# First attention of a two-block transformer kernel: turns, scores and values in one visit behind every second slab

## The reference

```
s = einsum('bnqhd,bnkhd->bhnqk', q, kb) * scale + rel_bias_band(rel_table)
s = where(valid, s, NEG_INF)
p = softmax(s, axis=-1)
o = einsum('bhnqk,bnkhd->bnqhd', p, vb)
```

## Time and profile before

| | us |
|---|---|
| three runs | 929.07, 929.38, 929.80 |
| median | 929.38 |
| profiled execution | 929.6 |
| its span | 927.8 |
| busy: TensorE, VectorE, ScalarE, GpSimd | 919.3, 599.4, 490.1, 303.6 |

### The profile page before, as it was taken

How to read it: one execution, slowest core, us unless ns; L and a number is a source line. 1 busy time by engine, 2 the same in 40 slices (tenths; PEclk the granted TensorE clock), 3 DMA queues, 4 the chain that set the end, 5 groups by cost and what they waited for, 6 DMA issues and landing times.

```text
span 927.8 us, 16744 instructions
## 1 busy us (share of the span) xinstructions
PE 919.3 (99%) x6268; PEld 833.8 (90%) x6268; DVE 599.4 (65%) x849; ACT 490.1 (53%) x765; POOL 303.6 (33%) x140
## 2 busy tenths in 40 slices
PE   9999999999999999999999999999999999999997
PEld 8999877788899999888999998888889889999886
DVE  6968967756657777723777775357476866666523
ACT  6788456743555444444644444446364754445441
POOL 0000000000044554544254556554341044445442
PEclk9999999999999999999999999999999999999999
DMA  8756575445556567796566666645513356666661
GB/s 258 248 182 183 175 230 179 133 159 185 178 170 194 182 188 235 238 257 197 182 189 197 195 209 203 222 151 159 175 63 93 113 153 190 196 199 190 189 200 67
DMA packets 132797, 169.49 MB, mean 183 GB/s; under 512 B 16731, under 2 KB 88446, under 8 KB 132614
## 3 DMA queue, kind: packets, MB, share of 16 engines
q1 hardware_dynamic: 132582, 168.67, 58.6%
q10 hardware_dynamic: 160, 0.07, 0.0%
HBM read 167.61 MB, written 1.10 MB: 182 GB/s over the span
## 4 chain that ended last, share of the span: by engine, by line
PE 92%; DVE 3%; issue 1%; DMA 1%; ACT 1%; SPq 1%; POOL 1%; DVEq 0%; POOLq 0%; ACTq 0%
PE acc L904 14%; PE acc L906 14%; PE acc L905 14%; PE acc L962 14%; PE acc L964 14%; PE acc L966 14%; PE tp L980 3%; PE acc L1315 1%; DVE w_lo L1400 1%; DMA w_raw<-in_w_ffn_out 1%; PE sc L1270 1%; PE sc L1116 1%; PE tp L1135 1%; PE acc L1048 1%; POOL w_lo L2068 1%
## 5 line engine op out<-in xcount | busy, mean ns | idle before, releaser
L541 ACT ACTIVATE w_hi<-w_raw 128x1024 fp32r<-128x1024 f32 x300 | 316.8, 1058 | 277.1 <-PE acc L906 130.0
L2068 POOL TENSOR_TENSOR w_lo<-w_raw,w_hi 128x1024 fp32r<-128x1024 f32 x106 | 278.4, 2626 | 512.4 <-ACT w_hi L541 512.3
L1400 DVE TENSOR_TENSOR w_lo<-w_raw,w_hi 128x1024 fp32r<-128x1024 f32 x194 | 258.0, 1334 | 200.6 <-ACT w_hi L541 200.1
L962 PE MATMUL acc<-xt_hi,w_hi 128*128 128x256 f32 x1248 | 347.4, 278 | 0.1
L966 PE MATMUL acc<-xt_hi,w_lo 128*128 128x256 f32 x1248 | 346.4, 278 | 0.0
L964 PE MATMUL acc<-xt_lo,w_hi 128*128 128x256 f32 x1248 | 346.4, 278 | 0.0
L962 PEld LDWEIGHTS acc<-xt_hi,w_hi 128*128 128x128 f32 x1248 | 235.2, 188 | 1.4 <-issue 0.9
L966 PEld LDWEIGHTS acc<-xt_hi,w_lo 128*128 128x128 f32 x1248 | 234.6, 188 | 0.0
L964 PEld LDWEIGHTS acc<-xt_lo,w_hi 128*128 128x128 f32 x1248 | 234.4, 188 | 0.1
L904 PE MATMUL acc<-w_hi,hid_hi 128*128 128x512 f32 x264 | 103.2, 391 | 0.1
L905 PE MATMUL acc<-w_hi,hid_lo 128*128 128x512 f32 x264 | 102.9, 390 | 0.0
(11 more groups left out here) (228 smaller groups left out, 949.7 us busy)
## 6 DMA issues: line engine op xcount, KB each, us to landing
w_raw<-in_ffn_w_gu SPq DMA_DIRECT2D x172, 256.0 KB
w_raw<-in_w_in SPq DMA_DIRECT2D x68, 512.0 KB
w_raw<-in_w_ffn_in SPq DMA_DIRECT2D x88, 256.0 KB
w_raw<-in_ffn_w_down SPq DMA_DIRECT2D x44, 512.0 KB
w_raw<-in_w_ffn_out SPq DMA_DIRECT2D x22, 512.0 KB
w_raw<-in_w_rnn_out SPq DMA_DIRECT2D x8, 512.0 KB
w_raw<-in_w_attn_out SPq DMA_DIRECT2D x8, 512.0 KB
w_raw<-in_w_o SPq DMA_DIRECT2D x8, 512.0 KB
```

The source lines that it names most:

```text
L541: act.activation(w_hi(q), w_raw[:, b, :], ACT.Copy).then_inc(hi_done[b], 1)
L962: pe.matmul(o, w_hi(s + q)[:, cols], xt1_hi[:, k, :], start=q == 0 and c == 2 * b and j == 0, stop=False, skip_group_check=True)
L1400: dve.tensor_tensor(w_lo(q), w_raw[:, b, :], w_hi(q).bitcast(F32), ALU.subtract).then_inc(lo_done[b], 1)
L2068: pool.tensor_tensor(w_lo(q), w_raw[:, b, :], w_hi(q).bitcast(F32), ALU.subtract).then_inc(lo_done[b], 1)
```

## The change

TensorE visits the attention behind slabs 1 and 3 only. Visit k (0 to 7) holds the turns of pair k, then the scores of pair k+1, then the values of pair k-1. The values of pair 7 keep their place behind the first slab of the next group. The values are written to sc[0] and sc[1], columns 384 to 511, in place of tp. The waits follow: the turns no longer wait for o_drained, the scores and values do; ScalarE waits for the values of pair k-1 (pv_done) before it overwrites pt1 with pair k. On ScalarE `values_hi1` moves behind `probs_T1`, for the odd pairs also behind a slab's `feed`; on VectorE `values_lo1` moves behind one `feed`, and then stands directly ahead of the eviction.

```diff
+                    if k > 0:
+                        act.wait_ge(pv_done, k)
                     act.activation(pt1[:, hh, :], tp[x % 2][:, 0:384], ACT.Copy).then_inc(tp_free[x % 2], 1)
...
-                    act.activation(at_hi[:, k, m * P:(m + 1) * P], tp[m][:, 384:512], ACT.Copy).then_inc(at_hi_done, 1)
+                    act.activation(at_hi[:, k, m * P:(m + 1) * P], sc[m][:, 384:512], ACT.Copy).then_inc(at_hi_done, 1)
...
                 exps1(k)
                 feed(s, 1)
+                probs_T1(k)
                 if k > 0:
                     values_hi1(k - 1)
-                probs_T1(k)
                 feed(s + 1, 1)
                 exps1(k + 1)
-                values_hi1(k)
                 feed(s + 2, 1)
                 probs_T1(k + 1)
+                values_hi1(k)
                 feed(s + 3, 1)
...
+                if k > 1:
+                    pe.wait_ge(o_drained, 2 * k - 2)
...
-                    pe.wait_ge(o_drained, 2 * k + hh + 1)
                     turn(X["p1"] + 2 * k + hh, [(P * n, sb1[:, hh, P * n:P * (n + 1)]) for n in range(3)])
...
+                pe.wait_ge(o_drained, 2 * k + 2)
...
-                        mm = pe.matmul(tp[m][HD * hh:HD * hh + HD, 384:512], u[:, 4, kt, head * HD:(head + 1) * HD],
+                        mm = pe.matmul(sc[m][HD * hh:HD * hh + HD, 384:512], u[:, 4, kt, head * HD:(head + 1) * HD],
...
+            def visit1(k):
+                turn_probs1(k)
+                if k + 1 < KT:
+                    scores1(k + 1)
+                if k > 0:
+                    values1(k - 1)
+
             for g in range(4):
...
-                after = {1: first_round, 2: lambda k=k: values1(k), 3: second_round}
-                if k > 0:
-                    after[0] = lambda k=k: values1(k - 1)
-                group(40 + 4 * g, 10 + g, XT1, 4, after=after)
+                group(40 + 4 * g, 10 + g, XT1, 4, after={1: lambda k=2 * g: visit1(k), 3: lambda k=2 * g + 1: visit1(k)})
...
                 normalise1(k)
+                feed(s, 1)
                 if k > 0:
                     values_lo1(k - 1)
-                feed(s, 1)
                 maxima1(k + 1)
                 feed(s + 1, 1)
                 normalise1(k + 1)
+                feed(s + 2, 1)
                 values_lo1(k)
-                feed(s + 2, 1)
```

More of the change, by code:

```diff
@@ L1141, in _ @@
             scores1(0)
-            for g in range(4):
[L1143 to L1152, removed]
-                after = {1: first_round, 2: lambda k=k: values1(k), 3: second_round}
-                if k > 0:
-                    after[0] = lambda k=k: values1(k - 1)
-                group(40 + 4 * g, 10 + g, XT1, 4, after=after)
+            def visit1(k):
[4 more added lines that the diff above has]
+                    values1(k - 1)
+            for g in range(4):
+                group(40 + 4 * g, 10 + g, XT1, 4, after={1: lambda k=2 * g: visit1(k), 3: lambda k=2 * g + 1: visit1(k)})
             pe.wait_ge(yt_ready, 1)
@@ L1647, in values_lo1 @@
                     cols = slice(m * P, (m + 1) * P)
-                    dve.tensor_tensor(at_lo[:, k, cols], tp[m][:, 384:512], at_hi[:, k, cols].bitcast(F32),
+                    dve.tensor_tensor(at_lo[:, k, cols], sc[m][:, 384:512], at_hi[:, k, cols].bitcast(F32),
                                       ALU.subtract).then_inc(o_drained, 1)
```

## The result

| | before | after |
|---|---|---|
| median of the runs compared, us | 929.24 | 933.12 |
| profiled span, us | 927.8 | 930.9 |
| first attention, from the first scores' start to the start of the values of pair 7, us | 67.71 | 71.12 |
| TensorE busy over the whole span, us | 919.3 | 919.2 |

A forecast was written before the change was run, and what follows sets the result against it. TensorE, busy 919.3 of 927.8 us, was taken as the bound. Saving 1.3 us by the merge and losing 4.4 in waits gave +3.1: 932.7 for the profiled execution, 932.5 as median, range 930.3 to 935.2.

The forecast's parts named there:

- The merge saves 1.3 us: TensorE, first attention: each of six visits holding turns, scores and values takes 2.51 us against 2.72, saving 0.21.
- the step from scores to values: TensorE inside a merged visit: no row showed it; values were taken to start 0.08 us before the scores' end.
- The bound of 2.3 us: TensorE's largest saving from the merge, if values could start 0.25 us before the scores' end: 0.38 per visit.
- The chain is 1.46 us too long, three times: Values' end to next even pair's normalised rows: 7.34 us against TensorE's 5.88, delaying turns of pairs 2, 4, 6.
- the 4.4 forecast: Total TensorE loss in us from waits at the turns of pairs 2, 4 and 6: 3 x 1.46.
- Even visits have 0.36 us to spare: After even visits the chain lacks the eviction: 5.52 us against 5.88, so the odd pairs' turns don't wait.
- the 5.88 that TensorE takes: TensorE's time in us from the values' end over two slabs to the second head's turn, when normalised rows are needed.
- A (covered): Rival, first attention: the chain causes no TensorE wait, only the saving remains, 928.1 us; chance 6%.
- B (even visits late): Rival, first attention: the chain after even visits is late too, so odd pairs' turns also wait; 936.8 us; chance 8%.
- C (the clock): Rival, TensorE: its clock drops in the new waits, each of three costing 1.7 us more; 937.6 us; chance 3%.

The follow-up runs named there:

- both: Changed kernel with VectorE's eviction ahead of at_lo and ScalarE's last w_hi ahead of the pt1 copies: ratio 0.9992 to the kernel before, stage 67.16 us.
- all ahead: Changed kernel with ScalarE's last w_hi ahead of the pt1 copies, VectorE's eviction, last w_lo and next maxima ahead of at_lo: 928.03 us, ratio 0.9982 to before.
- tp banks: Changed kernel with the values written to the tp banks again, as in the kernel before: ratio 1.0041 to the kernel before, stage 71.10 us.
- values first: Changed kernel with values in the tp banks and, inside a visit, ahead of the scores: ratio 1.0011 to the kernel before, stage 68.54 us.
- two buffers: Changed kernel with a second buffer for pt1, so copies need not wait for the previous pair's values: ratio 1.0010 to before, stage 68.65 us.

## Why the prediction was right

| stage against the kernel before, us | expected | measured |
|---|---|---|
| changed kernel | +3.1 | +3.41 |
| eviction ahead of at_lo | +1.5 | +1.59 |
| w_hi ahead of the copies | as changed | +3.40 |
| both | -0.6 | -0.55 |
| all ahead | -1.3 | -1.41 |
| tp banks | as changed | +3.39 |
| values first | +0.8 | +0.83 |
| two buffers | +1.0 | +0.94 |

**The merge saves 1.3 us.** Held: 1.41, seen by itself in the version without waits ("all ahead"). The open point was the step from scores to values. It pays like its neighbours: the values start 0.08 before the end of the scores and not 0.25. This is in line with the rule of the Trainium skill ("TensorEngine Tiling (Array Packing)", "Key Properties") that a change of the tiling mode drains the array; no run varies the mode by itself. The bound of 2.3 us falls.

**The chain is 1.46 us too long, three times.** Held: the waits stand at the three places named, behind the steps named. Term by term, from the rows above, it measures: values' end (140.97 + 0.88 = 141.85) to the copies 0.11, forecast 0.04; copies 0.76; at_hi to at_lo 0.31; at_lo 0.41; eviction 1.32; w_lo 1.13; maxima to exponential 0.67; to the reciprocal 1.02; to the end of the scalings 1.63; to TensorE 0.05. Together 7.41 against 7.34. The eviction starts 1.59 us after the values' end, where some 1.5 were named. With the stage 1.41 shorter by the merge and 3.41 longer in the end, the waits are worth 4.82, or 1.61 each. Of the difference to 1.46, 0.07 is the chain's first step, the one term that was set a little small, and 0.06 is that the scores start 0.48 after the second head's turns (149.26 to 149.74) in place of 0.42 in a block without a wait. The remaining 0.02 is not traced. The waits cost 0.4 us more than the 4.4 forecast and the merge saves 0.1 more than its 1.3, so that the two errors cancel in part.

**Even visits have 0.36 us to spare.** Held: the turns of pairs 3, 5 and 7 do not wait. The last scaling ahead of the turns of pair 3, in VectorE's timeline:

```profile
156.15 0.56 DVE L1637 TENSOR_SCALAR sb<-sb,inv 128x128 f32<-128x128 f32 x2
```

From the values' end (150.59 + 0.88 = 151.47) to 156.71 and 0.05 more are 5.29 us, 0.59 less than the 5.88 that TensorE takes, so there was a little more to spare. The scalings had been put at 1.62 at most; from the first reciprocal (155.30) to their end they take 1.41.

**Rivals.** A (covered) and B (even visits late) are ruled out by the timeline. C (the clock) did not come about: over the stage of the changed kernel TensorE's granted clock is full, in the table by stretches (busy us and instructions of each engine, granted clock, share of DMA, GB/s):

```profile
125.68:196.80 71.12, 67.65 (x401) 51.68 (x401) 47.98 (x152) 46.21 (x119) 0.00 (x0) 1.00 0.47 148
```

TensorE is idle for 3.47 of the 71.12 us, and the clock stays at 1.00. The Trainium skill ("TensorE: Matmul & The Clock Gate", "A second HAM failure mode: psum-queue depth-cycling") tells of short idle spells that made the clock fall and rise in another kernel. The six spells here, of 0.82 and 0.33 us, have no such effect.

**The median.** 933.12 against 932.5 is 0.6 off, and the range of 930.3 to 935.2 holds it. 0.3 of this is the stage. What is left is not explained.

## What to carry to other kernels

When work is moved later on the engine that bounds the kernel, look at what stands at the head of the other engines' queues when it comes late: here two engines stood still for some 4 us with ready work behind one operation, and moving that work ahead turned 3.9 us lost into 1.6 won. A chain worked out term by term from the trace of before, against the time that TensorE takes over the slabs between, gave the size of the wait to 0.15 us. Two things in one queue can each hide the other, so an edit that gives nothing alone (0.01 us) may be half of a pair that gives 4.

## What was not expected

An idle bracket understates a wait of TensorE: 0.82 and 0.33 us stand for 0.99 and 0.55 us of later starts, since the products overlap in the profile by 0.17 and more. So TensorE's busy time in the stage is the same as before (67.65 against 67.71 us) although the merge saves 1.41: in the version without waits it is 66.30. The waits cost 4.82 us, of which 3.47 show as idle and the rest as less overlap. A wait of 0.28 us does not show as idle at all, only as a block of turns of 1.10 in place of 0.82 us.
